# First block's input projections in column pairs by seven products, one modulation part per pair, and order changes elsewhere

## What is computed

```python
mod = silu(c) @ ada_w[layer] + ada_b[layer]             # six vectors: shift, scale, gate, twice
h = modulate(rmsnorm(x, norm1_w[layer]), shift1, scale1)
# layer 0
u, q, k, v = split(h @ mix_w_in, 4)                     # 1024 x 2048: 16 column blocks of 128
a_out = pool_mixer(u);  b_out = chunk_attention(q, k, v, rel_bias)
x = x + gate1 * (concat(a_out, b_out) @ mix_w_out)
# layer 1: Mamba-2 mixer, 8 groups of heads
z, xbc, dt = split(h @ ssm_w_in)                        # per group g: B, C, x0, x1, z0, z1
... conv, silu, scan ...;  g = y * silu(z);  g = g * rsqrt(mean(g * g) per group) * norm_w
x = x + gate1 * (g @ ssm_w_out)
# after each: a mixture of experts; then the second block, untouched here
```

## Time and profile before

| | |
|---|---|
| median of 3 runs | 3528.21 us (3522.74 to 3529.82) |
| the profiled execution's own time | 3523.41 us |
| its span, first to last instruction | 3521.4 us |
| mean granted TensorE clock | 0.976 |
| PE busy | 3288.0 us (93%) |
| DVE busy | 1768.3 us (50%) |
| ACT busy | 897.9 us (25%) |
| POOL busy | 245.1 us (7%) |
| SP's queue q1 | 348.01 MB, 31.3% of 16 engines |

### The profile page before, as it was taken

The page is one execution under the profiler, slowest core; times in us unless marked ns, Lnnn a source line. Parts: engine busy times, 40 slices in busy tenths (PEclk is TensorE's granted clock), DMA queues, the critical chain, the costliest instruction groups (busy, mean ns, idle before and its releaser), DMA issues.

```text
span 3521.4 us, 36361 instructions
## 1 busy us (share of the span) xinstructions
PE 3288.0 (93%) x13360; PEld 2051.3 (58%) x13360; DVE 1768.3 (50%) x3325; ACT 897.9 (25%) x1843; POOL 245.1 (7%) x218
## 2 busy tenths in 40 slices
PE   7979897999998998988999999999989899999998
PEld 3443553777734654555555555555544556778886
DVE  1153334877723336868434453344467854554554
ACT  2041122333321222045222121111111523222222
POOL 0000430432200430000000000000000000000000
PEclk9999898999999998999999999999999999999999
DMA  8837786323256874101111211222122011223331
GB/s 278 258 107 245 293 315 208 103 81 93 78 170 221 306 281 119 42 12 35 48 36 39 57 48 54 60 59 61 56 65 66 13 58 48 72 61 88 86 88 62
DMA packets 418493, 393.98 MB, mean 112 GB/s; under 512 B 27888, under 2 KB 353648, under 8 KB 410896
## 3 DMA queue, kind: packets, MB, share of 16 engines
q1 hardware_dynamic: 384768, 348.01, 31.3%
q10 hardware_dynamic: 15120, 23.68, 2.0%
q0 software_dynamic: 18432, 19.98, 1.7%
HBM read 440.78 MB, written 31.52 MB: 134 GB/s over the span
## 4 chain that ended last, share of the span: by engine, by line
PE 80%; DVE 5%; ACT 4%; DMA 3%; issue 2%; SPq 0%; ACTq 0%; DVEq 0%; POOL 0%; POOLq 0%
PE psum L690 37%; PE psum L675 9%; PE psum L1036 7%; PE psum L888 5%; PE psum L1137 3%; PE psum L907 2%; PE psum L1233 2%; ACT arena L1515 2%; DVE arena L2066 2%; PE psum L1281 2%; DMA ring<-in_w_branch 1%; PE psum L873 1%; PE psum L1301 1%; PE psum L1313 1%; PE psum L780 1%
## 5 line engine op out<-in xcount | busy, mean ns | idle before, releaser
L690 PE MATMUL psum<-arena,ring 128*128 128x384 f32 (+1 forms) x2592 | 746.0, 438 | 13.7 <-DVE arena L2063 5.3
L690 PEld LDWEIGHTS psum<-arena,ring 128*128 128x128 f32 x2592 | 491.6, 190 | 238.9 <-DVE psum L2063 12.3
L690 PE MATMUL psum<-hT,ring 128*128 128x384 f32 (+1 forms) x2176 | 623.6, 440 | 2.0 <-ACT part_sum L1515 2.0
L690 PEld LDWEIGHTS psum<-hT,ring 128*128 128x128 f32 x2176 | 414.0, 190 | 191.4 <-issue 6.9
L675 PE MATMUL psum<-hT,ring 128*128 128x512 f32 (+1 forms) x1056 | 415.0, 553 | 16.8 <-DVE hT L2059 14.5
L1515 ACT ACTIVATE part_sum<-psum 128x256 f32<-128x256 f32 (+1 forms) x387 | 166.8, 432 | 921.0 <-PE psum L690 806.5
L1515 ACT ACTIVATE arena<-psum 128x512 f32<-128x512 f32 (+5 forms) x501 | 210.1, 466 | 571.1 <-PE psum L675 300.0
L2063 DVE TENSOR_TENSOR ring<-ring 128x512 f32<-128x512 f32 (+1 forms) x336 | 215.9, 662 | 258.1 <-PE psum L690 255.5
L675 PEld LDWEIGHTS psum<-hT,ring 128*128 128x128 f32 x1056 | 202.8, 194 | 229.0 <-issue 214.1
L2063 DVE TENSOR_TENSOR psum<-psum,part_sum 128x256 f32<-128x256 f32 (+1 forms) x307 | 146.7, 482 | 330.4 <-PE psum L690 276.3
L1507 ACT ACTIVATE arena<-psum,cols 128x256 f32<-128x256 f32 (+3 forms) x280 | 132.5, 494 | 637.6 <-PE psum L888 193.9
(11 more groups left out here) (250 smaller groups left out, 3539.3 us busy)
## 6 DMA issues: line engine op xcount, KB each, us to landing
ring<-in_w_in SPq DMA_DIRECT2D x172, 512.0 KB, 4.1
arena<-in_moe_w SPq DMA_DIRECT2D x44, 1536.0 KB
ring<-in_ada_w SPq DMA_DIRECT2D x96, 512.0 KB, 6.5
ring<-in_w_mod SPq DMA_DIRECT2D x48, 512.0 KB, 6.4
ring<-in_ssm_w_in SPq DMA_DIRECT2D x48, 512.0 KB, 5.3
ring<-in_w_branch SPq DMA_DIRECT2D x64, 256.0 KB, 3.2
hT<-in_moe_w SPq DMA_DIRECT2D x10, 1536.0 KB
ring<-in_moe_w SPq DMA_DIRECT2D x10, 1024.0 KB
```

The source lines that it names most:

```text
L690: mm = nc.tensor.matmul(flat(bank_, nb), lhs[:, k, :], rhs(k), start=(start and k == 0), stop=(k == kd_ - 1), skip_group_check=True)
```

## The change

1. Stage A: columns 0 and 1 stay direct; columns 2 to 15 become seven pairs ("A", 1) to ("A", 7) of the seven-product scheme, with a modulation part between Q6 and Q3 of each pair. Quads 1 and 2 take these eight places (one after column 0, seven in the pairs); their bank is bank 7, kept out of the turn of the others meanwhile (`kept`). The pooling of VectorE moves between the sums.
2. Quad 7 moves into layer 1: its parts lie in pairs 0, 1 and 2 of group 1 and pair 0 of group 2, again with bank 7 kept, which lasts from group 1's first pair to the scores of group 2.
3. Layer 1's loop: the group norm's logarithm and exponential (`group_log`, `group_root`) move from the group's end to the next group, behind two exponentials of 1280 columns; both `z_gate` and both `z_full` come right after the squares; the scaling of y (`y_normed`) moves behind a later `seg`.
4. Layer 1's output projection: quad 5's parts lie before columns 4 to 7 and no longer 3 to 6.
5. `bias_load(0)` and `bias_load(1)` are issued before stage A.

```diff
-        QUAD_INA = {2: (1, 0), 3: (1, 1), 4: (1, 2), 5: (1, 3), 7: (2, 0), 8: (2, 1), 9: (2, 2), 10: (2, 3),
-                    12: (7, 0), 13: (7, 1), 14: (7, 2), 15: (7, 3)}
+        QUAD_INA = {0: (1, 0), 1: (1, 1), 2: (1, 2), 3: (1, 3), 4: (2, 0), 5: (2, 1), 6: (2, 2), 7: (2, 3)}
+        QUAD_PAIR = {(1, 0): (7, 0), (1, 1): (7, 1), (1, 2): (7, 2), (2, 0): (7, 3)}
...
+                    if st["kept"] and name[1] == "quad":
+                        b = BANKS - 1
+                    else:
+                        if st["kept"] and st["j"] % BANKS == BANKS - 1:
+                            st["j"] += 1
+                        b = st["j"] % BANKS
+                        st["j"] += 1
...
-            for c in range(16):
-                if c in QUAD_INA:
-                    quad_part(*QUAD_INA[c])
+            st["kept"] = True
+            for c in range(2):
                 linear(("inA", c), lambda k: hT[:, k, :], ready="n1_0" if c == 0 else None)
...
+            for i in range(1, 8):
+                pair_head("A", i)
+                if i > 1:
+                    pair_tail("A", i - 1)
+                if i == 4:
+                    quad_turn(1)
+                pair_middle("A", i, lambda: quad_part(*QUAD_INA[i]))
+            st["kept"] = False
...
                     pair_head(g + 1, 0)
-                    pair_middle(g + 1, 0)
+                    pair_middle(g + 1, 0, beside(0))
                     pair_head(g + 1, 1)
                     pair_tail(g + 1, 0)
-                    pair_middle(g + 1, 1)
+                    pair_middle(g + 1, 1, beside(1))
                     ssm_y(g, 0)
...
-                if i in QUAD_INA:
-                    quad_put(*QUAD_INA[i])
                 put(block8(w, P * c))
+                if i != 1 and (i == 0 or i % 2):
+                    quad_put(*QUAD_INA[i // 2])
...
                     seg_exp(4 * g)
                     seg_exp(4 * g + 1)
+                    if g:
+                        group_log(g - 1)
                     if g < 7:
                         part_copy(g + 1, 0, 1)
+                    if g:
+                        group_root(g - 1)
+                    if g < 7:
                         part_copy(g + 1, 0, 3)
                         part_copy(g + 1, 0, 2)
...
                     if g < 7:
                         z_gate(g + 1, 0)
-                    inv_root(("g", g), 4 * 256, col("eps"))
-                    if g < 7:
                         z_gate(g + 1, 1)
...
-                    if c < 7:
-                        quad_part(5, c - 3)
+                    if c >= 4:
+                        quad_part(5, c - 4)
                     out_part(c, 0, 16)
...
+            bias_load(0)
+            bias_load(1)
```

More of the change, by code:

```diff
@@ L333, in program @@
         win = [arena[:, win_at + (S + 16) * i:win_at + (S + 16) * (i + 1)] for i in range(2)]
+        mH = Arena(at=mA.at, end=MODW - 2 * D)
+        T_inA = mH.take(3, 4, S // 2)
+        inA_sums = [mH.take(12, P) for _ in range(2)]
         mE = Arena()
@@ L632, in _ @@
             held = {}
-            st = {"j": 0, "l": 0, "names": []}
+            st = {"j": 0, "l": 0, "names": [], "kept": False}
             def job(*name):
@@ L926, in moe, with half_product @@
                     mm.then_inc(tensor_done, pe.step(full))
+            two = {}
+            def half_product(bank_, lhs, rhs, start, name):
+                for k in range(4):
+                    mm = nc.tensor.matmul(bank_[:, 0:S // 2], lhs[:, k, :], rhs(k), start=(start and k == 0), stop=(k == 3),
+                                          skip_group_check=True)
+                mm.then_inc(tensor_done, pe.step(name))
+            low = lambda h: lambda k: hT[:, k, S // 2 * h:S // 2 * h + S // 2]
@@ new lines, in _, with pair_head @@
+            high = lambda h: lambda k: hT[:, 4 + k, S // 2 * h:S // 2 * h + S // 2]
+            total = lambda g, j: lambda k: (T_inA if g == "A" else T_ssm)[:, j, k, :]
+            def pair_head(g, n):
+                a_, b_ = pair_jobs(g, n)
+                wa, wb = take(("wa", g, n)), take(("wb", g, n))
+                x = job(*b_[1:])
+                half_product(x[0], wa[0][:, 0:4, :], low(0), True, ("Q1", g, n))
+                w = job(*a_[1:])
+                half_product(w[0], wa[0][:, 4:8, :], high(0), True, ("Q2", g, n))
+                two[g, n] = wa, wb, x
@@ L1030, in _ @@
                 quad_turn(6)
[L1031 to L1047, removed]
-                    x = job("ssm", g, b_, "x")
-                    half_product(x[0], wa[0][:, 0:4, :], low(0), True, ("Q1", g, n))
-                    w = job("ssm", g, a_, "x")
-                    half_product(w[0], wa[0][:, 4:8, :], high(0), True, ("Q2", g, n))
-                    two[g, n] = wa, wb, x
@@ L2224, in _ @@
                 v.tensor_copy(up[:, g, 16:S], other[:, 32:16 + S]).then_inc(vector_done, ve.step(("pooled", g)))
-            quad_add(1)
-            quad_add(2)
-            quad_add(7)
+            for i in range(1, 8):
+                c11("A", i)
+                if i >= 4:
+                    pooling(i - 4)
+                c12("A", i)
+                c22("A", i)
+                if i in (4, 7):
+                    quad_add(1 if i == 4 else 2)
             def pool_out():
@@ L3145, in pair_sums @@
                 g_.tensor_tensor(wb[:, 0:4, :], wa[:, 0:4, :], wb[:, 0:4, :], ALU.subtract).then_inc(gpsimd_done, po.step(("S3", "ssm", g, n)))
+            for i in range(1, 8):
+                pair_sums("A", i)
             if stage_on(2):
```

226 lines of the change are left out of this document (140 added, 86 removed).

## The result

| | kernel before | changed kernel |
|---|---|---|
| median, measured side by side, 4 runs each | 3525.89 us | 3573.01 us (3569.90 to 3576.74) |
| ratio, 95% interval | | 1.0135, 1.0122 to 1.0148 |
| span of the profiled execution | 3521.4 us | 3574.3 us |
| mean granted clock of TensorE | 0.976 | 0.965 |

What follows compares the result with a forecast made beforehand. The prediction took TensorE's work and waits (80% of the span) to bound the kernel. Its terms summed to +30.5 us on a median of 3528.2 us, giving 3559 us, 0.9% slower, with a range of 3527 to 3577 us.

Steps and rivals of the forecast that it cites:

- 1. products saved: Stage A: seven pairs of half products replace fourteen direct columns and save TensorE work, -12.9 us.
- 2. ring, stage A: Stage A, pairs 2 to 7: TensorE waits 5.1 us each for the part's four transfers, issued after the tail; +29.7 us.
- 2. part (7, 1): Layer 1, group 1, pair 1: the same wait for a part's transfers occurs once, +5.1 us.
- 2. old wait: Stage A: the one DMA wait of the kernel before goes, -0.9 us.
- 3. clock, stage A: Stage A: half clock behind each of six transfer waits costs 1.5 us, +9.0 us.
- 4. ss bank: Layer 1's pair heads: six waits for a bank freed late by the logarithm, +22.0, less 14.6 for waits before cb 2.
- 4. clock: Layer 1's loop: half clock behind the six head waits, less 3.4 us behind the removed waits; net +4.4 us.
- 5. output projection: Layer 1's output projection: waits for a part (2.1 us) and column 3's weights (3.4 us) go, -5.5 us.
- 6. bias: Attention's first softmax: the wait for the bias transfer goes, 6.4 us, with 0.9 of half clock; -7.3 us.
- Both rivals on the low side: Part's transfers hidden in stage A: 3514 us, chance 0.07; ss bank in layer 1's heads costs nothing: 3529 us, 0.08.
- The saving isn't there: Stage A rival: half products double the weight loads and the pairs gain nothing, 3572 us; chance 0.07.
- Worse: Rival: clock stays low most of a pair or POOL's sums come late, 3 to 5 us more for seven; chance 0.06.

Runs made afterwards that it cites:

- e1: Changed kernel with stage A's modulation part behind Q7 and the previous pair's tail right behind the part: 3534.14 us, ratio 1.0026 to the kernel before.
- e9: Changed kernel with product Q5 computed three times instead of once in pairs 2 to 7 of stage A: 3567.73 us, ratio 1.0112.
- e4: Changed kernel with the edits of e1, e2 and e3, and part (7, 1) moved behind ssm_y 0: 3493.98 us, ratio 0.9915.
- e2: Changed kernel with the group norm's logarithm back at its own group's end, between the two readings of z: 3544.20 us, ratio 1.0056.
- e8: Kernel before with change 4 alone (quad 5's parts before columns 4 to 7): 3518.49 us beside 3525.15, ratio 0.9980.
- e3: Changed kernel with the first two experts' weights transfer issued behind the weights of output column 4 in layer 1: 3565.10 us, ratio 1.0112.
- e7: Kernel before with change 5 alone (attention's bias loads issued before stage A): 3521.72 us beside 3525.15, ratio 0.9988.
- e10: Kernel before with changes 3 and 4 (group norm's new order, quad 5's parts moved): 3536.93 us beside 3524.49, ratio 1.0036.
- e6: Kernel before with change 3 alone (group norm in two steps, logarithm in the next group): 3534.26 us beside 3524.49, ratio 1.0024.
- e5: Changed kernel with stage A's modulation part moved behind Q7, the previous pair's tail left behind the next head: 3549.13 us, ratio 1.0066.

## Why the prediction was right, and where short

Forecast and measured, in us, each by the steps of the prediction:

| term | forecast | measured | from |
|---|---|---|---|
| 1. products saved | -12.9 | -12.1 | e1 against before to the softmax, -27.8, less 5.8 at the softmax, 1.0 of column 0's clock, old wait 1.0, quad 7's four parts and turn 8.3, and 0.4 for a short new wait |
| 2. ring, stage A | +29.7 | +27.9 | waits of the changed kernel |
| 2. part (7, 1) | +5.1 | +4.8 | the same |
| 2. old wait | -0.9 | -1.0 | before |
| 3. clock, stage A | +9.0 | +11.3 | e1 less column 0; e9 |
| 3. clock, part (7, 1) | +1.5 | +2.5 | loop of e4 (339.3) against e2 (346.6), less 4.8 |
| 4. ss bank | +22.0 - 14.6 | +21.7 - 14.6 | waits |
| 4. clock | +7.8 - 3.4 | +11.2 - 3.4 | e2 |
| 5. output projection | -5.5 | -6.7 alone, +8 on top with change 3 | e8, e3 |
| 6. bias | -7.3 | -4.6 | e7, to the end of attention |

The measured terms make 45.0 us of the 47.1; 2.1 are unexplained, less than what the interval of the ratio (1.3 parts in a thousand either way) leaves open.

The measured 3573 us lie in the stated range, 4 us below its upper end. That is partly luck: three terms (clock, output projection and bias) erred by 16 us together, all in one direction, and it was the width of the range that took it up.

**Right.** The direction, both main mechanisms and nearly each size of theirs: six ring waits (27.9 for 29.7), two heads at 4.8 us and four at 3.0 with the bank as the reason (21.7 for 22.0), and the saving of the products. Both rivals on the low side fell by the trace: no transfer was hidden, and the logarithm never ended before the head. Two rivals gave times as near to 3573 us as the forecast or nearer, so the time alone doesn't decide against them. *The saving isn't there* (3572 us) falls by e1, where the products save 12.1 us. *Worse* (3580 to 3595) falls by its mechanism: no wait for POOL's sums is there, and the clock cost 1.9 us for each ring wait in stage A, not 1.5 and 3 to 5 more. One bound of the forecast doesn't follow from its own working: with 4.0 us for the first transfer and 1.35 for each of three more, less 3.45 of cover, the lower bound of one wait is 4.6 us and not 4.2. ScalarE: Activation LUTs (What ACT_TABLE_LOAD costs) of the Trainium skill would have added a drain to each of the six waits, 8.3 us together as an estimate from its figure; the trace doesn't agree, since the logarithm at 710.04 us starts 0.02 us after its load has ended, and the six stay at the sum without it.

**Mis-sized: the clock.** "I take 1.5 us for a wait of about 5 us" was too small: 11.3 over six waits is 1.9 us each, and in the heads it was 1.7 where I had 1.2 and 2.2 where I had 1.5. I had read it off one long wait and seven short ones of which two were followed by half clock. The step that failed is this carrying over of one row and a share to waits of 3 to 5 us: in this kernel each of the thirteen was followed by half clock. It isn't so by necessity, as the one wait of 3.01 us in e10 shows. Together 18.3 us forecast, 25.0 measured: 6.7 of the 16.6 us by which the sum of 30.5 fell short.

**Wrong: "-5.5" for the output projection in this kernel.** The term is right for change 4 alone (e8). I priced each change against the order of before. I named what SP's queue would do earlier for its own columns, but not what stands behind them in it, the experts' transfer, nor which small loads of ScalarE would then meet it; and I let the new place of `y_normed` cost nothing without asking whose lateness it would now inherit. That is -6.7 + 8 for -5.5: 6.8 us of the shortfall.

**Mis-sized: the bias.** 6.4 us were to go and 0.9 with the half clock behind the hole. TensorE's wait shrank by 5.8, because other work of VectorE still stands there, and the half clock behind the shorter wait fell on more of attention's products, 1.2 us the other way: -4.6 for -7.3, 2.7 us of the shortfall.

## What to carry to other kernels

When an order change frees a queue earlier, follow the queue past the transfers that you wanted: the next burst also comes earlier, and the small loads issued near it, by any engine, came 8.8 to 9.8 us after their issue here, instead of 4. When two changes meet in one place, price them in the order that holds with both. In this kernel's dense stretches a wait of 3 to 5 us on TensorE cost itself and, all but once, about 2 us of half clock, so six small waits are worth a move of one instruction: the same products with the tail, the logarithm and one transfer elsewhere gave 3486 us instead of 3573.

## What the hardware showed that I had not expected

- Useless products made the kernel faster: 20.8 us more of TensorE's work in stage A (e9), 7.7 us less time there, the granted clock between 70 and 190 us 1.00 instead of 0.90.
- Half clock followed each of the waits of 3.0 us in layer 1's heads in the changed kernel and in e6, and five of six in e10, where of the 2.1 us waits only two in seven had been followed by it; in e5 a part after 1.1 to 1.7 us of idle time ran at full speed, and in e9 after 2.7 us.
- A shorter wait gave back less than its length: with the hole before the first softmax 5.8 us shorter, the products behind it lost 1.2 us at half clock (e7).
- Two small loads of ScalarE landed 8.8 us (changed kernel) and 9.8 us (e10) after their issue at 1020.01 and 983.01 us, behind one column's weights (two slots) and two of the experts' transfers on another engine's queue; in e6, with no such burst before them, the segment started 3.8 us after the issue (983.94 to 987.75).
- The same burst of four transfers, from its issue to the part that needs it, took 7.9 to 8.6 us in four pairs of e5 and 10.65 in a fifth; in the changed kernel all six took 8.2 to 8.3.
